# Causal attention inside a decoder trunk: scores laid out with keys on partitions, a separate product pass for the row maxima, row sums by adds on GpSimd

## The chip, the cores and the metric

The kernel runs on one core of one Trainium2 chip. The metric is the device time of one execution in microseconds; the median of several runs counts. Engines: PE is TensorE, DVE is VectorE, ACT is ScalarE, POOL is GpSimd, SP is SyncE (here it only issues DMAs).

## The reference, cut to what matters

One layer on x (1, 2048, 1024) in float32: an input projection, three token mixers (pooling, attention with a forget gate, a state-space layer), gates, an output projection and a layer norm. The change touches the attention:

```python
logf = jax.nn.log_sigmoid(f_logit)                       # (B, S, 8 heads)
fcum = jnp.cumsum(logf, axis=1)
scores = einsum('bqhd,bkhd->bhqk', qi, k) / sqrt(64)     # head dim 64, S = 2048
bias = fcum[query] - fcum[key]                           # per head
logits = jnp.where(key_pos <= q_pos, scores + bias, -inf)
p = jax.nn.softmax(logits, axis=-1)
out = einsum('bhqk,bkhd->bqhd', p, v)                    # then * silu(gate), then w_up_b
...
gates = sigmoid(zg)     # 3 x 1024 columns of the input projection, each with K = 1024
```

## The kernel before

The kernel has three stages with a barrier of all engines between them: `stage_project` (to about 600 us), `stage_attend` (601 to 1530 us) and `stage_merge` (from 1530 us). Products run in fp32r. Every fp32 operand is split into a high half (an ACT copy to fp32r) and a low half (a DVE subtraction), and a product is done as three (high x high, high x low, low x high), or as two passes where both halves of one operand are stacked on partitions 0 to 63 and 64 to 127.

`stage_attend` works head by head. It also computes the gates' projection (24 tiles of 128 columns for each half of the tokens): per head 12 pieces of 24 products of 512 columns, 288 products, which `fill(slot)` spreads between the steps of the attention so that PE has work while other engines prepare its operands. `fill_plan()` fixes how many gate products stand in which slot. The order on each engine is written out by hand, the same order for every head; semaphores tie the engines together. Heads 0 to 3 are phase 0 and heads 4 to 7 phase 1; between the phases x is loaded and split again for the other half of the tokens (`high_x` L1387, `low_x` L1513).

Within a head a loop goes over 16 tiles t of 128 queries:

- `queries(t+1)` (L1566): the scores with queries on partitions, in pieces of up to 512 keys, two products each (k_hh, k_ll), into three banks `s_ps`.
- `logits` (L1451) on DVE: one operation per piece adds the bias of F (`f_row`, or `f_last` with the mask for the last 128 keys), writes the piece to `s_sb` and takes its row maxima; L1478 joins them to `neg_max`.
- `weights_of` (L1395) on ACT: one exp over the whole row with `neg_max` as bias, and with the row's sum as a second result.
- `turn` (L1576): the weights, 128x128 block by block, are transposed on PE (L1584) into `t_ps`; ACT copies the high half out (L1419), DVE subtracts the low half (L1543).
- `values` (L1588), for every two tiles: v (high half on output rows 0 to 63, low half on 64 to 127) times the weights of 256 queries, high and low, into `o_ps`; ACT copies the lower rows (L1366) and DVE adds them (L1481).
- Once per head the 16 row sums of each query are inverted (L1539, 128x16), transposed (L1603) and written to `invT` in HBM. The merge stage multiplies by them (`scale` in `split_y`, L1718).

At a head's end ACT and DVE split the next head's k and q (`split_kq`, L1374 and L1498). GpSimd computes nothing in this stage: it issues the DMAs for k, q, v, F and the outputs.

In `stage_merge` PE works through 8 blocks of 256 tokens: products into `u_ps` (L2063), gating, products into `h_ps` (L2090), layer norm.

Of the kernel before, what the change touches and what calls it, by code (L numbers as in the profile page):

```python
# [25 lines left out]
P = 128  # L26
# [48 lines left out]
class Kept:  # L75


    def __init__(self, nc, ctx, early_at):
# [30 lines left out]
        self.s_sb0 = at("s_sb0", 4, [P, S])  # L109
# [4 lines left out]
        self.y_out = [at(f"y_out{i}", 5, [P, 2 * P], skip=4 * (2 * BANK + i * 2 * P)) for i in range(2)]  # L114
# [11 lines left out]
        self.k_hh = nc.alloc_sbuf_tensor_at("k_hh", [P, S], F32R, offset=late_at)  # L126
# [12 lines left out]
        self.wu_high, self.wu_split, self.scaled = sem("wu_high"), sem("wu_split"), sem("scaled")  # L139
# [6 lines left out]
def stage_project(nc, io, scr, kept, ident, x_hi, x_lo, x_raw, w_hi, w_lo, w_raw):  # L146


    with ExitStack() as ctx:
# [3 lines left out]
        def sem(name):  # L153
# [49 lines left out]
        x_loaded = [sem(f"x_loaded{k}") for k in range(KT)]  # L203
# [8 lines left out]
         f_done, f_stored) = (  # L212
# [5 lines left out]
                "f_exp", "f_ln", "f_done", "f_stored"))  # L218
# [191 lines left out]
        def _(dve):  # L410
# [144 lines left out]
            for hf in range(2):  # L555
# [152 lines left out]
                next_split(2 + hf)  # L708
                if hf == 0:
# [231 lines left out]
        def _(pool):  # L941
# [108 lines left out]
            for hf in range(2):  # L1050
# [20 lines left out]
                if hf == 1:  # L1071
# [18 lines left out]
            pool.wait_ge(f_stored, 16)  # L1090


def fill_plan():

    per_piece = 3 * KT
    total = G_TILES * NCH * per_piece
    steps = [(t, j) for t in range(Q_TILES) for j in range(-(-(t + 1) // 4))]  # L1100
    slots = ["start", *steps, "end", "tail"]
    counts = {s: FILL_BETWEEN for s in steps}
    counts.update({"start": FILL_START, "end": FILL_END, "tail": FILL_TAIL})
    rest = total - sum(counts[s] for s in slots if isinstance(s, str) or s[1])

    rest -= sum(FILL_SHORT)
    for t in range(Q_TILES):
        counts[t, 0] = rest * (t + 1) // Q_TILES - rest * t // Q_TILES
    for t, more in enumerate(FILL_SHORT):
        counts[t, 0] += more  # L1110
    counts[Q_TILES - 2, 0] -= FILL_LAST
    counts[Q_TILES - 1, 0] += FILL_LAST
    ends, splits, done = {s: [] for s in slots}, {s: [] for s in slots}, 0
    splits["head"] = [1]
    for n, s in enumerate(slots):
        before, done = done, done + counts[s]
        for piece in range(before // per_piece, done // per_piece):
            ends[s].append(piece)
            if piece % NCH == NCH - 1 and piece // NCH + 2 <= G_TILES:
                at = W_SPLIT_AT.get(s[0])  # L1120
                splits[(at, 0) if at else "end"].append(piece // NCH + 2)
    assert done == total
    return counts, ends, splits


Q_TILES = S // P
PHASE_HEADS = HEADS // 2
G_TILES = T_GATE // PHASE_HEADS
FILL_SHORT = (9, 6)
W_SPLIT_AT = {1: 4, 5: 8, 9: 10, 12: 14}  # L1130
FILL_START, FILL_END, FILL_TAIL, FILL_BETWEEN, FILL_LAST = 30, 16, 22, 3, 3
S_PIECES = sum(-(-(t + 1) // 4) for t in range(Q_TILES))
PT_USES = 2 + S_PIECES


def stage_attend(nc, io, scr, kept, ident, mask, x_hi, x_lo, x_raw, gw_hi, gw_lo, gw_raw):
# [4 lines left out]
    with ExitStack() as ctx:  # L1141
# [3 lines left out]
        def sem(name):  # L1145
# [3 lines left out]
        sb("k_hh_place", [P, S])  # L1149
        k_hh = kept.k_hh  # L1150
        g_bias = kept.spare("g_bias", 1, [P, T_GATE])
        g_out, y_out = kept.g_out, [y[0:HD] for y in kept.y_out]
        inv_row = kept.y_out[0][HD:HD + Q_TILES, 0:P]
        k_ll, q_st, q_tmp, vT, f_row = kept.k_ll, kept.q_st, kept.q_tmp, kept.vT, kept.f_row
        v_st = sb("v_st", [P, Q_TILES, 2 * HD], F32R)
        s_sb = [kept.s_sb0, sb("s_sb1", [P, S])]
        mx = [kept.spare(f"mx{i}", 3, [P, 5], 32 * i) for i in range(2)]
        f_last = sb("f_last", [P, P])
        neg_max = [kept.spare(f"neg_max{i}", 3, [P, 1], 64 + 32 * i) for i in range(2)]
        row_sum = kept.spare("row_sum", 0, [P, Q_TILES])  # L1160
        row_inv = kept.spare("row_inv", 0, [P, Q_TILES], 4 * Q_TILES)
        o_low = sb("o_low", [HD, 2 * P])
        pt_hi = sb("pt_hi", [P, Q_TILES, 2 * P], F32R)
        assert nc.sbuf_base <= kept.wu_at + 4 * (KT - EARLY_SPLIT) * KT * P
        pt_lo = sb("pt_lo", [P, Q_TILES, 2 * P], F32R)

        s_ps = [ctx.enter_context(nc.psum_tensor(f"s_ps{i}", [P, BANK], F32)) for i in range(3)]
        t_ps = [ctx.enter_context(nc.psum_tensor(f"t_ps{i}", [P, BANK], F32)) for i in range(2)]
        o_ps = ctx.enter_context(nc.psum_tensor("o_ps", [P, 2, 2 * P], F32))
# [6 lines left out]
        y_stored, y_free = sem("y_stored"), sem("y_free")  # L1176
        x2_loaded = [[sem(f"x2_loaded{c}_{k}") for k in range(0, KT, 2)] for c in range(NCH)]
        x_lo_used, early_loaded = sem("x_lo_used"), sem("early_loaded")
        (x2_hi, x2_split, gb_loaded, gb_half, gw_split_hi, gw_split, g_done, g_ready, k_hi,
         kq_low, f_masked, q_hi, s_full, s_free, max_ready, p_ready, t_full, t_hi, t_lo, inv_ready, o_full,  # L1180
         o_low_ready, y_ready) = (
            sem(n) for n in (
                "x2_hi", "x2_split", "gb_loaded", "gb_half", "gw_split_hi", "gw_split", "g_done", "g_ready", "k_hi", "kq_low", "f_masked", "q_hi", "s_full", "s_free", "max_ready",
                "p_ready", "t_full", "t_hi", "t_lo", "inv_ready", "o_full", "o_low_ready", "y_ready"))

        kq_loaded, v_loaded, f_loaded = kept.kq_loaded, kept.v_loaded, kept.row_loaded

        def pieces(t):

            n0 = sum(-(-(a + 1) // 4) for a in range(t))  # L1190
            keys = (t + 1) * P
            return [(n0 + j, j * BANK, min(BANK, keys - j * BANK)) for j in range(-(-keys // BANK))]
# [5 lines left out]
        def pieces_to(t):  # L1198

            return pieces(t)[-1][0] + 1  # L1200

        gates = scr["gateT"].rearrange("(g d p) t -> d p g t", g=3, p=P)
        assert nc.sbuf_base <= kept.wu_at + 4 * (KT - EARLY_SPLIT + 1) * KT * P
# [3 lines left out]
        def _(sp):  # L1207
# [5 lines left out]
            def store(row, now, m2, c):  # L1213
# [3 lines left out]
                             g_out[c][:]).then_inc(g_stored[c], 16)  # L1217

# [6 lines left out]
            for phase in range(2):  # L1225
# [8 lines left out]
                if phase == 1:  # L1234

                    sp.wait_ge(t_full, (HEADS - 1) * PT_USES + 2)
                    sp.wait_ge(y_stored, 16 * ((HEADS - 1) * 9 + 2))
                    load_inv(sp, kept, scr, 0)
                    for i in range(EARLY):
                        sp.dma_start(kept.early_raw[:, i].rearrange("p k c -> p (k c)"), io["w_up"][i]  # L1240
                                     ).then_inc(early_loaded, 16)
                for u in range(2):
                    for c in range(NCH):
# [11 lines left out]
                        if phase == 1 and u == 0 and c == 1:  # L1255
                            sp.wait_ge(s_full, HEADS * S_PIECES)
                            sp.wait_ge(y_stored, 16 * ((HEADS - 1) * 9 + 2))
                            for g in range(YG):
                                for dst, src in ((kept.mix[g], scr["mixT"]), (kept.sil[g], scr["silT"])):
                                    rows = src[g * (D // YG):(g + 1) * (D // YG)].rearrange("(k p) t -> p k t", p=P)  # L1260
                                    sp.dma_start(dst[:], rows[:, :, 0:BLOCK]).then_inc(kept.mix_loaded[g], 16)
                            sp.wait_ge(g_stored[0], 16 * (T_GATE + 2 * KT + 2))
                            sp.dma_start(kept.gate0[:], gates[0][:, :, 0:BLOCK]).then_inc(kept.gate_loaded[0], 16)
# [970 lines left out]
```

## Time and profile before

| | |
|---|---|
| median of 3 runs | 1898.52 us (1897.03 to 1898.54) |
| span of the profiled execution | 1897.9 us |
| PE busy | 1880.5 us, 99% |
| DVE busy | 1123.9 us, 59% |
| ACT busy | 720.4 us, 38% |
| POOL busy | 450.8 us, 24% |
| mean granted TensorE clock | 0.998 |
| `stage_attend` | 601 to 1530 us |

The times are of runs without a profile. The profiled execution has no time of its own beside its span, from its first to its last instruction; the median is 0.6 us above that. "Busy" is time in which at least one instruction of the engine is under way. PE's products overlap (the next one starts before the last one's result has drained), so the cost of a product is the distance between two starts.

### The profile page before, as it was taken

What the parts mean: (1) busy time and instruction counts of PE and PEld (TensorE: products, weight loads), DVE (VectorE), ACT (ScalarE), POOL (GpSimd) and SP (SyncE); (2) the same over time, 40 slices, a digit from 0 to 9 for tenths busy, and PEclk for the clock granted to TensorE, in tenths of its full rate; (3) what the DMA queues carried; (4) which work ended last, traced back from release to release, by engine and by line L of the source; (5) the groups of instructions that cost most, each with busy time, mean ns of one, the idle gap of its engine ahead of it and who ended that gap; (6) DMA issues with size and microseconds to landing.
All of it is one profiled execution on the core that took longest, in us unless ns stands there. A gap on an engine that the chain in (4) does not pass through costs nothing. (4 is left out here: it accounts for less than half of the span.)

```text
span 1897.9 us, 30532 instructions
## 1 busy us (share of the span) xinstructions
PE 1880.5 (99%) x10349; PEld 1611.9 (85%) x10349; DVE 1123.9 (59%) x2370; ACT 720.4 (38%) x1105; POOL 450.8 (24%) x595
## 2 busy tenths in 40 slices
PE   9999999999999999999999999999999999999998
PEld 7888887888887888888888788888888889999997
DVE  5554225564235665746656675565656688766776
ACT  3121013111024565555545655555555542121111
POOL 2948920399000000010100001000010002223322
PEclk9999999999999999999999999999999999999999
DMA  7132235322432143161432714224152486666542
GB/s 197 67 101 89 88 111 186 80 89 89 151 128 100 63 128 85 45 158 57 126 82 68 228 51 133 77 77 131 49 153 74 157 294 199 189 180 183 166 133 89
DMA packets 111335, 230.22 MB, mean 121 GB/s; under 512 B 11544, under 2 KB 61320, under 8 KB 107640
## 3 DMA queue, kind: packets, MB, share of 16 engines
q1 hardware_dynamic: 96752, 168.69, 27.7%
q0 software_dynamic: 13920, 59.46, 11.9%
q10 hardware_dynamic: 576, 1.05, 0.2%
q8 instruction: 38, 0.62, 0.1%
q14 instruction: 49, 0.40, 0.1%
HBM read 159.29 MB, written 69.27 MB: 120 GB/s over the span
## 5 line engine op out<-in xcount | busy, mean ns | idle before, releaser
L1628 PE MATMUL g_ps<-x_hi,w_hi 128*128 128x512 f32 x768 | 305.9, 398 | 0.0
L1628 PE MATMUL g_ps<-x_hi,w_lo 128*128 128x512 f32 x768 | 305.6, 398 | 0.0
L1543 DVE TENSOR_TENSOR pt_lo<-t_ps,pt_hi 128x512 fp32r<-128x512 f32 (+2 forms) x320 | 193.2, 610 | 150.0 <-ACT pt_hi L1419 145.3
L1628 PE MATMUL g_ps<-x_lo,w_hi 128*128 128x512 f32 x768 | 231.7, 406 | 1.2 <-PEq L1664 1.2
L1419 ACT ACTIVATE pt_hi<-t_ps 128x512 fp32r<-128x512 f32 (+2 forms) x320 | 170.6, 533 | 154.8 <-PE t_ps L1584 149.2
L763 PE MATMUL tile_ps<-x_hi,w_hi 128*128 128x512 f32 x720 | 223.7, 392 | 0.1
L763 PE MATMUL tile_ps<-x_hi,w_lo 128*128 128x512 f32 x720 | 221.8, 389 | 0.0
L763 PE MATMUL tile_ps<-x_lo,w_hi 128*128 128x512 f32 x720 | 221.8, 389 | 0.0
L1306 POOL DMA_DIRECT2D mixT<-y_out x63 | 33.8, 536 | 678.5 <-DVE y_out L1487 601.0
L1584 PE MATMUL t_ps<-ident,s_sb 128*128 128x128 f32 x1088 | 173.1, 274 | 2.5 <-DVE v_st L1528 2.5
L1464 DVE CUSTOM_DVE_ANT_0 s_sb<-s_ps,f_row 128x512 f32<-128x512 f32 (+3 forms) x288 | 161.1, 597 | 15.0 <-PE s_ps L1573 15.0
L323 ACT ACTIVATE w_hi<-w_lo_raw 128x1024 fp32r<-128x1024 f32 x47 | 49.9, 1061 | 312.3 <-DMA w_lo_raw<-in_w_tiles 312.3
L1628 PEld LDWEIGHTS g_ps<-x_hi,w_lo 128*128 128x128 f32 x768 | 144.8, 189 | 25.3
L1628 PEld LDWEIGHTS g_ps<-x_hi,w_hi 128*128 128x128 f32 x768 | 145.1, 189 | 24.7
L1398 ACT ACTIVATE s_sb<-s_sb,neg_max 128x128 f32<-128x128 f32 (+15 forms) x128 | 153.3, 1198 | 24.7 <-DVE neg_max L1478 24.6
L1584 PEld LDWEIGHTS t_ps<-ident,s_sb 128*128 128x128 f32 x1088 | 131.9, 140 | 36.2 <-DVE v_st L1528 3.0
L763 PEld LDWEIGHTS tile_ps<-x_hi,w_hi 128*128 128x128 f32 x720 | 134.6, 188 | 29.4 <-issue 1.4
L763 PEld LDWEIGHTS tile_ps<-x_lo,w_hi 128*128 128x128 f32 x720 | 135.2, 188 | 28.2
L763 PEld LDWEIGHTS tile_ps<-x_hi,w_lo 128*128 128x128 f32 x720 | 135.2, 188 | 28.1
L1628 PEld LDWEIGHTS g_ps<-x_lo,w_hi 128*128 128x128 f32 x768 | 137.0, 190 | 23.3 <-PEq L1664 1.3
L2063 PE MATMUL u_ps<-y_hi,wu_hi 128*128 128x256 f32 x512 | 144.1, 281 | 0.8 <-PEq L1141 0.8
L2063 PE MATMUL u_ps<-y_lo,wu_hi 128*128 128x256 f32 x512 | 144.5, 282 | 0.0
(319 smaller groups left out, 3595.5 us busy)
## 6 DMA issues: line engine op xcount, KB each, us to landing
w_lo_raw<-in_w_tiles SPq DMA_DIRECT2D x95, 512.0 KB, 3.7
gateT<-g_out SPq DMA_DIRECT2D x96, 256.0 KB, 3.0
gate<-gateT SPq DMA_DIRECT2D x62, 384.0 KB, 4.7
qkvT<-zout SPq DMA_DIRECT2D x24, 512.0 KB, 3.2
x_lo_raw<-in_xT SPq DMA_DIRECT2D x20, 512.0 KB, 9.7
silT<-zout SPq DMA_DIRECT2D x16, 512.0 KB, 2.7
k_ll<-qkvT POOLq DMA_DIRECT2D x16, 512.0 KB, 7.3
q_st<-qkvT POOLq DMA_DIRECT2D x16, 512.0 KB, 9.2
```

Source lines behind the costliest of these rows:

```text
L323: act.activation(w_hi[par][:], w_raw[par][:], ACT.Copy).then_inc(w_split_hi, 1)
L763: last = pe.matmul(tile_ps[par][:, c * BANK:(c + 1) * BANK], w[par][:, k, :], x[:, k, c * BANK:(c + 1) * BANK], start=(k == 0 and j == 0), ...
L1306: pool.dma_start(scr["mixT"][bass.ds(row, HD), p * 2 * P:(p + 1) * 2 * P], y_out[p % 2]).then_inc(y_stored, 16)
L1398: act.activation(row, row, ACT.Exp, bias=neg_max[t % 2][:], accum_out=row_sum[:, t:t + 1]).then_inc(p_ready, 1)
L1419: act.activation(pt_hi[:, k0 // P:(k0 + keys) // P, (t % 2) * P:(t % 2 + 1) * P], t_ps[n % 2][:, 0:keys].rearrange("p (k q) -> p k q", q=P ...
L1464: return dve.tensor_tensor_reduce(s_sb[t % 2][:, k0 + a:k0 + b], s_ps[n % 3][:, a:b], f, 1.0, -3e38, ALU.subtract, ALU.max, mx[t % 2][:, c ...
L1543: dve.tensor_tensor(pt_lo[part], t_ps[n % 2][:, 0:keys].rearrange("p (k q) -> p k q", q=P), pt_hi[part].bitcast(F32), ALU.subtract).then_i ...
L1584: last = pe.transpose(t_ps[n % 2][:, a * P:(a + 1) * P], s_sb[t % 2][:, k0 + a * P:k0 + (a + 1) * P], ident[:])
L1628: mm = pe.matmul(g_ps[c][:], w[j % 2][:, k, :], x[:, k, c * BANK:(c + 1) * BANK], start=(r == 0), stop=(r == 3 * KT - 1))
L2063: mm = pe.matmul(u_ps[d % 2][:, n, :], w, y[:, k, :], start=(k == k0 and j == 0), stop=(k == k1 - 1 and j == 2))
```

## The change

Scores come with keys on partitions, so that the weights need no transpose before the values. 16 query tiles become four groups g of 512 queries (`Q_GROUPS`, `QG` = 4); a head has 40 steps (g, i), one per group and tile of 128 keys.

- `maxima(g, m)`: one product of the high halves (q_m as weights, k_b moving), with queries on partitions, only to get a row maximum. DVE reduces it in `s_ps` (`tensor_reduce`, and `tensor_tensor_reduce` with the mask for the last 128 keys). It needs to be no exact maximum, since the same shift is applied everywhere. `shifts`: three small DVE operations; `shift_rows`: one PE transpose, and four DVE copies into rows 64 and 65 of q_m, where the shift enters the scores' product as two more rows; F of the keys enters as rows 96 and 97 of k_b. The pieces for group g+1 stand in the steps of group g (`MAX_COUNTS`).
- `scores(n)`: two products (k_b x q_m, k_a x q_low) of up to 512 queries into `st_ps[n % 2]`. `weights` on ACT: exp from `st_ps` to a slot of `p_all` (three slots). `masked` on GpSimd: affine_select on the diagonal block. `high_p` (ACT copy) and `low_p` (DVE subtraction, both inputs in SBUF).
- `add_up` on GpSimd: sums p_all over the key tiles into `acc`. `sums(g)` on PE: ones times acc, high and low, into one of the two banks `s_ps`. Every use of `s_ps` (maxima, shift transposes, sums; `bank_order`) alternates between them.
- `values(n - 2)`: two products into `o_ps[g % 2]`. `low_rows`, `output`: as before, 64x512. `inverse(g)` on DVE: reciprocal of 64x512 out of `s_ps` into `inv`. `scale_y` on GpSimd multiplies, `store_y` stores; no `invT`, and no `scale` in the merge.
- At a head's end: four ACT copies (`high_kq`, before `low_rows` of the last group) and two DVE operations (`low_kq`). In front of the first head begins now wait for the last store of qkvT, and v is loaded only then. F is stored negated and split, by two DVE operations in the projection stage.

```diff
+LAG, RING_P = 2, 3
+FILL_A, FILL_B, FILL_C, FILL_END, FILL_MID, FILL_TAIL = 10, 10, 10, 12, 8, 14
+FILL_SHORT = 8
+MAX_COUNTS = ((3, 3, 2, 0), (2, 2, 2, 2, 2, 2, 0, 0), (2, 2, 2, 2, 2, 2, 1, 1, 1, 1, 0, 0), (0,) * 16)
+def last_step(g):
+    return 2 * (g + 1) * (g + 2) - 1
+SUM_AT = {last_step(g) + LAG + 2: g for g in range(Q_GROUPS - 1)}
...
+            def maxima(at, g, m):                       # PE
+                pe.wait_ge(s_free, at(S_USES, u + 1))
+                pe.matmul(s_ps[u % 2][:, 0:keys], q_m[:, t * P:(t + 1) * P], k_b[:, k0:k0 + keys], start=True,
+                          stop=True).then_inc(s_full, 1)
+            def sums(at, g):                            # PE
+                pe.wait_ge(s_free, at(S_USES, u + 1))
+                pe.wait_ge(acc_split, at(Q_GROUPS, g + 3))
+                pe.matmul(s_ps[u % 2][:], ones[:], acc_hi[:], start=True, stop=False)
+                pe.matmul(s_ps[u % 2][:], ones[:], acc_lo[:], start=False, stop=True).then_inc(s_full, 1)
+            def inverse(at, g):                         # DVE
+                dve.wait_ge(y_ready, at(Q_GROUPS, g + 1))
+                dve.wait_ge(s_full, at(S_USES, u + 1))
+                dve.reciprocal(inv[:], s_ps[u % 2][0:HD]).then_inc(s_free, 1)
+            def low_p(at, n):                           # DVE
+                dve.wait_ge(p_high, at(N_STEPS, n + 1))
+                dve.tensor_tensor(p_lo[:, n % RING_P, q0:], p_all[:, n % RING_P, q0:], p_hi[...], ALU.subtract)
...
+                fill("A")                               # PE, one head
+                # 16 transposes of v
+                for m in range(QG):
+                    maxima(at, 0, m)
+                fill("B")
+                shift_rows(at, 0)
+                fill("C")
+                for n, (g, i) in enumerate(STEPS):
+                    scores(at, n)
+                    if n in SUM_AT:
+                        sums(at, SUM_AT[n])
+                    for m in pieces_at(n):
+                        maxima(at, g + 1, m)
+                    if n == last_step(g) and g + 1 < Q_GROUPS:
+                        shift_rows(at, g + 1)
+                    fill(n)
+                    if n >= LAG:
+                        values(at, n - LAG)
+                fill("end")
+                values(at, N_STEPS - 2)
+                fill("mid")
+                values(at, N_STEPS - 1)
+                sums(at, Q_GROUPS - 1)
+                fill("tail")
...
+                for n, (g, i) in enumerate(STEPS):      # DVE, one head
+                    if n in SUM_AT:
+                        inverse(at, SUM_AT[n])
+                    for m in pieces_at(n):
+                        maxima(at, g + 1, m)
+                    if n:
+                        low_p(at, n - 1)
...
-                    last = pe.transpose(t_ps[n % 2][:, a * P:(a + 1) * P], s_sb[t % 2][...], ident[:])
-                dve.reciprocal(row_inv[:, 0:t + 1], row_sum[:, 0:t + 1]).then_inc(inv_ready, 1)
```

## Rows read from the trace of the kernel before

**Rows 1.** The page: busy time and share of an engine; chain that ended last.
```profile
PE 1880.5 (99%) x10349; PEld 1611.9 (85%) x10349; DVE 1123.9 (59%) x2370; ACT 720.4 (38%) x1105; POOL 450.8 (24%) x595
...
PE u_ps L2063 9%; PE h_ps L2090 8%; PE h_ps L2099 1%; DMA gate<-gateT 0%; DVE wo_lo L1929 0%; DVE gate L1988 0%; DVE wu_lo L1929 0%; DVE gate_first L1988 0%; DVE gate L1996 0%; DVE m_lo L1941 0%; DVE x_t L2040 0%; DVE gate L2000 0%; DVE gate_first L1996 0%; DVE x_t L2047 0%; PE h_ps L2080 0%
```

**Rows 2.** Windows, attention: stretch, length, PE, PEld, DVE, ACT, POOL busy, clock, DMA, GB/s.
```profile
601.00:1530.00 929.00, 926.46 (x5323) 795.93 (x5324) 574.01 (x1598) 524.35 (x849) 62.32 (x113) 1.00 0.36 105
```

**Rows 3.** Timeline of PE, 760 to 764 us: start, duration, line, count.
```profile
760.87 0.39 PE L1628 MATMUL g_ps<-x_hi,w_hi 128*128 128x512 f32 x1
761.10 0.28 PE L1598 MATMUL o_ps<-pt_hi,v_st 128*128 128x256 f32 x1
761.21 0.28 PE L1598 MATMUL o_ps<-pt_lo,v_st 128*128 128x256 f32 x1
...
762.94 0.62 PE L1584 MATMUL t_ps<-ident,s_sb 128*128 128x128 f32 x4
763.32 0.47 PE L1628 MATMUL g_ps<-x_hi,w_lo 128*128 128x512 f32 x1
763.63 0.39 PE L1628 MATMUL g_ps<-x_hi,w_hi 128*128 128x512 f32 x1
```

**Rows 4.** Timeline of PE, the transposes of v in two consecutive heads.
```profile
723.56 1.21 PE L1645 MATMUL t_ps<-ident,vT 64*128 64x64 f32 x16
...
839.08 1.21 PE L1645 MATMUL t_ps<-ident,vT 64*128 64x64 f32 x16
```

**Rows 5.** DVE groups, 620 to 1545 us (count | busy us, mean ns), and one timeline row.
```profile
L1543 DVE TENSOR_TENSOR pt_lo<-t_ps,pt_hi 128x512 fp32r<-128x512 f32 x224 | 154.9, 692 | 113.0 <-ACT pt_hi L1419 108.4
...
L1448 DVE TENSOR_TENSOR w_lo<-w_lo_raw,w_hi 128x1024 fp32r<-128x1024 f32 x46 | 56.3, 1224 | 36.9 <-ACT w_hi L1352 36.9
...
L1464 DVE CUSTOM_DVE_ANT_0 s_sb<-s_ps,f_last 128x128 f32<-128x128 f32 x124 | 35.6, 287 | 26.9 <-PE s_ps L1573 26.3 <-DVE f_last L1456 0.6
...
L1539 DVE RECIPROCAL row_inv<-row_sum 128x16 f32<-128x16 f32 x8 | 2.0, 253 | 11.4 <-ACT s_sb L1398 11.4
...
L1539 DVE RECIPROCAL row_inv<-row_sum 128x2 f32<-128x2 f32 x1 | 0.2, 155 | 0.0
...
581.51 1.28 DVE L663 TENSOR_SCALAR zout<-tile_ps,bias 128x1024 f32<-128x1024 f32 x1 [5.05 <-PE tile_ps L763]
```

**Rows 6.** ACT groups, 620 to 1545 us.
```profile
L1376 ACT ACTIVATE k_hh<-k_ll 128x2048 fp32r<-128x2048 f32 x7 | 13.3, 1902 | 0.0
```

**Rows 7.** DMA issues (KB each, us to landing), and a memset of POOL.
```profile
qkvT<-zout SPq DMA_DIRECT2D x24, 512.0 KB, 3.2
...
vT<-qkvT POOLq DMA_DIRECT2D x8, 512.0 KB, 4.7
...
L1044 POOL MEMSET toep<- 128x2048 f32 x1 | 1.8, 1814 | 0.0
```

**Rows 8.** Timeline of PE and windows (the clock after POOL's column) at the phase change.
```profile
1078.31 0.33 PE L1584 MATMUL t_ps<-ident,s_sb 128*128 128x128 f32 x1 [2.54 <-DVE v_st L1528]
...
1078.30:1079.50 1.20, 1.20 (x6) 1.09 (x7) 1.20 (x6) 0.28 (x1) 0.00 (x0) 1.00 0.41 157
1079.50:1082.90 3.40, 3.40 (x9) 2.62 (x8) 1.37 (x10) 1.18 (x3) 0.00 (x0) 0.50 0.25 90
1082.90:1090.00 7.10, 7.10 (x40) 5.95 (x39) 3.52 (x15) 3.24 (x8) 0.54 (x1) 1.00 0.29 90
```

**Rows 9.** POOL adds in the merge, and POOL beside DVE in the projection (timeline).
```profile
L2117 POOL TENSOR_TENSOR x_t<-x_t,ln_b 128x512 f32<-128x512 f32 x30 | 40.0, 1353 | 1.2
...
187.38 0.91 POOL L1029 TENSOR_TENSOR xs<-xs,zs 128x256 f32<-128x256 f32 x1
188.24 1.89 POOL L1030 TENSOR_TENSOR xw<-xw,scratch 128x256 f32<-128x256 f32 x1
...
187.89 1.47 DVE L421 TENSOR_TENSOR w_lo<-w_lo_raw,w_hi 128x1024 fp32r<-128x1024 f32 x1 [3.12 <-ACT w_hi L323]
```

More of the change, by code:

```diff
@@ L1099, in fill_plan @@
     total = G_TILES * NCH * per_piece
[L1100 to L1112, printed above, removed]
+    slots = ["A", "B", "C", *range(N_STEPS), "end", "mid", "tail"]
+    counts = {"A": FILL_A, "B": FILL_B, "C": FILL_C, "end": FILL_END, "mid": FILL_MID, "tail": FILL_TAIL}
+    for n in range(QG):
+        counts[n] = FILL_SHORT
+    rest, steps = total - sum(counts.values()), N_STEPS - QG
+    for n in range(QG, N_STEPS):
+        counts[n] = rest * (n - QG + 1) // steps - rest * (n - QG) // steps
     ends, splits, done = {s: [] for s in slots}, {s: [] for s in slots}, 0
-    splits["head"] = [1]
-    for n, s in enumerate(slots):
+    splits[1] = [1]
+    for s in slots:
         before, done = done, done + counts[s]
@@ L1119, in fill_plan @@
             if piece % NCH == NCH - 1 and piece // NCH + 2 <= G_TILES:
-                at = W_SPLIT_AT.get(s[0])
-                splits[(at, 0) if at else "end"].append(piece // NCH + 2)
+                later = s + SPLIT_LATER if isinstance(s, int) else "tail"
+                splits[later if later in splits else "end"].append(piece // NCH + 2)
     assert done == total
     return counts, ends, splits
[L1126 to L1133, printed above, removed]
 def stage_attend(nc, io, scr, kept, ident, mask, x_hi, x_lo, x_raw, gw_hi, gw_lo, gw_raw):
@@ L1158, in stage_attend @@
[L1158 to L1167, printed above, removed]
@@ new lines, in stage_attend @@
+        acc_hi, acc_lo = sb("acc_hi", [P, BANK], F32R), sb("acc_lo", [P, BANK], F32R)
+        o_low = sb("o_low", [HD, BANK])
+        y_t = [sb("y_t0", [HD, BANK]), kept.y_last]
+        inv = sb("inv", [HD, BANK])
+        p_hi = sb("p_hi", [P, RING_P, BANK], F32R)
+        p_lo = sb("p_lo", [P, RING_P, BANK], F32R)
+        p_all = sb("p_all", [P, RING_P, BANK])
+        assert nc.sbuf_base <= kept.wu_at + 4 * (KT - EARLY_SPLIT + 1) * KT * P
+        g_bias = kept.spare("g_bias", 1, [P, T_GATE])
@@ L1182, in stage_attend @@
             sem(n) for n in (
[L1183 to L1192, printed above, removed]
+                "x2_hi", "x2_split", "gb_loaded", "gb_half", "gw_split_hi", "gw_split", "g_done", "g_ready", "made", "rows_made", "rows_zero",
@@ L1234, in _ @@
                 if phase == 1:
[L1236 to L1241, printed above, removed]
+                    load_merge()
                 for u in range(2):
@@ L1254, in _ @@
                             load_wo(sp, kept, io["w_out"], 0)
[L1255 to L1263, printed above, removed]
-                            sp.wait_ge(t_full, (HEADS - 1) * PT_USES + pieces_to(Q_TILES - 2) + 2)
-                            sp.wait_ge(g_stored[0], 16 * (T_GATE + 2 * KT + 4))
-                            for d, place in kept.gate_first.items():
-                                sp.dma_start(place[:], gates[d][:, :, 0:BLOCK]).then_inc(kept.gate_loaded[d], 16)
                         if phase == 0 and u == 1 and c == 1:
@@ L1545, in body @@
+                low_p(at, N_STEPS - 1)
+                low_acc(at, Q_GROUPS - 1)
                 for j in splits("end", last):
@@ L1565, in _ @@
         def _(pe):
-            def queries(at, t, part=slice(None)):
-                for n, k0, keys in pieces(t)[part]:
-                    if n >= 3:
-                        pe.wait_ge(s_free, at(S_PIECES, n - 2))
-                    ps = s_ps[n % 3][:, 0:keys]
-                    pe.matmul(ps, q_st[:, t * P:(t + 1) * P], k_hh[:, k0:k0 + keys], start=True, stop=False)
-                    last = pe.matmul(ps, q_st[:, t * P:(t + 1) * P], k_ll[:, k0:k0 + keys], start=False, stop=True)
-                    last.then_inc(s_full, 1)
```

755 lines of the change are left out of this document (429 added, 326 removed).

## The prediction

> **What bounds the kernel now.** First the page's busy shares and the chain that ended last: TensorE (PE) is busy 99% of the span, VectorE (DVE) 59%, and the chain is TensorE's products [rows 1]. Then the windows: in the attention stretch, the only one the change rewrites, PE is busy 926 of 929 us, DVE 574, ScalarE 524, GpSimd 62 [rows 2]. "Busy" doesn't say what a product costs, since neighbours overlap; start to start does [rows 3]. A 512-column fp32r product takes 0.23 us, a 256-column one 0.11 to 0.12, so I take 0.17 for 384 and 0.06 for 128. Four 128-column transposes take 0.38 and make the next product 0.08 late: 0.115 each. One head lasts 839.08 - 723.56 = 115.5 us [rows 4]. Its sum: 288 gate products 66.2, scores (two passes over 17,408 columns) 15.7, values 16.4, 16 transposes of v 1.1, and 16.1 left for 137 transposes. PE is full, so each wait the change adds is paid in full.
>
> **TensorE's work.** A pass over the causal triangle in the new steps is 24 products of 512 columns and four sets of 512, 384, 256 and 128: 24 x 0.23 + 4 x 0.58 = 7.8 us. Per head: gates 66.2, scores 15.7, values 15.7, the new maxima pass 7.8, four row sums of two products 1.8, four transposes of shifts 0.5, v 1.1: 108.8. That saves 6.7 a head; 8 x 108.8 = 870.
>
> **VectorE's work.** What it does to 512 columns takes 0.69, to 128 0.29, to 1024 1.22, so a column costs 1.04 ns [rows 5]. No row shows a long tensor_reduce; one input at one column per step gives 0.69 for 512, and I know no row below that. The exception is the reciprocal. Before, it handles 16 columns a head in 0.253 us; with 2 columns it takes 0.155 [rows 5]: 0.098 for 14 columns, 7.0 ns a column. The change inverts the sum for each of 512 queries, copied over 64 partitions, four times a head: 0.155 + 510 x 0.0070 = 3.7 us each. Bounds: 0.69 (like the other operations) and 4.3; I take 3.7, since both rows are of this very operation. The Trainium skill ("VectorE: DVE Perf Modes", The fixed hardware budget) says that the reciprocal runs through the pipe with a repeat count of 8; 8 x 1.04 ns x 512 would be 4.3 us as an estimate, and the forecast some 15 us later. The row agrees in kind (6.7 times a normal column).
>
> DVE per head: lower halves of the weights 24 x 0.69 + 4 x 1.97 = 24; maxima 24 full pieces, 16 masked ones of 128 columns (0.29 and 0.08 for the result) and what lies beside these, 27; reciprocals 15; splits of six w tiles, k, q and v 7.3 + 4.4 + 1.4 = 13; outputs and sums 8 x 0.69 = 6; shifts 6: 91 us. That is less than 108.8, but unevenly spread, and DVE works in order.
>
> **Where PE stops.** The maxima, the shift transposes and the sums share two banks in turn, and each use waits until DVE is through with the use two before.
> - Steps 7 and 15 (the sums of groups 0 and 1): PE does the sum, one maxima product, and for the next it needs the bank of the sum, so the reciprocal must end. It starts 0.39 after the second sum product starts and lasts 3.7, with 0.2 for two handovers and some backlog: 4.3; PE has 0.46 of work. Stop 4.0. Behind it wait the gate products, the values and the next scores. 16 x 4.0 = 64.
> - Step 27 (group 2's sum, no maxima): the lower half of step 26 is ready 5.65 after the step begins, PE wants it at 4.3 (step 27 takes 2.6, then 0.46 of scores and 1.23 of gates): 1.4 each, 11 in all. The reciprocal ends at 4.95 there, the subtraction takes 0.69.
> - Steps 0 and 1 issue three maxima products at once for two banks: 0.7 + 0.5 a head, 10.
> - End of a head, T = last scores. ScalarE splits w, does a gate at T+4.6, then four copies of 2048 columns for the next q and k at 1.9 each [rows 6] to T+12.3, and only then o_low to 12.9. DVE: output 13.6, reciprocal 17.4. PE has end, mid, tail and A fills and v's transposes to T+13.7; its second maxima product needs the sum's bank: 3.6. Then DVE splits v (1.4) before the first maxima, so the third and fourth products wait 1.6 and 0.6. 5.8 a head; 6 x 5.8 = 35.
> - Phase change: the new x is split on DVE after that reciprocal, 16 x 0.69, and the third maxima product waits behind all of it. A's products wait for the first split to T+18.1 (8 late), the maxima to T+29.8 (8 more): 16.
> - First head: q, k and v wait for the last qkvT store, which takes 3.2, and v's load another 4.7 [rows 7], against 30 gate products as cover before and 10 now; two memsets of GpSimd at 1.8 stand ahead of v's load. v lands at about 609.7, where PE is through with its cover at 603.2. ScalarE's four copies, from 603.9 on, end at 611.5 and its copy of v at 612.7, DVE's half of v at 613.4, and PE then issues the fourth maxima product at 614.5, 10 later than it could: 10.
> - Last head: PE's warm products wait for the last reciprocal: 2.
>
> **The clock.** Before has one stop of this kind: PE idle 2.54 us at the phase change; 1.2 us after it has restarted the granted clock is 0.50 (1.2 GHz) for 3.4 us, then 1.00 again [rows 8]. That costs 1.7. Stops of 4 us should do the same: 16 at steps 7 and 15, 6 at heads' ends and 2 at the first head and the phase change: 24 x 1.7 = 41. Bounds: nothing, and more than one fall in the long ones (+10).
>
> **What costs nothing.** GpSimd: an add of 512 columns takes 1.35 [rows 9]. Per head 24 of them (32), the 16 shorter ones (14), 16 masks of 128 columns at no more than 0.9 (14), four multiplications (5) and the DMAs (5) are 70 us of 108.8; the three slots of p_all give it two steps of slack. ScalarE has an exp and a copy per step, 1.3 us; a step of PE is 2.15 to 2.6. Were the adds twice as slow, they would set the steps of group 3 (2.7 against 2.15): some 8 us a head. The two operations on F in the projection (2048 columns, 2.2 each) fit in the 5.05 us that DVE idles behind them [rows 5]; without it they would delay a tile by 4.4 once. In the merge two multiplications a block go from DVE, where PE's products are the chain [rows 1]: nothing.
>
> **Sum.** 870 + 10 + 64 + 11 + 35 + 16 + 10 + 2 + 41 = 1059 against 929 now [rows 2]: +130. The profiled execution spans 1897.9, the median is 1898.5, 0.6 above: 1898.5 + 130 = 2028 us.
>
> **The rivals.**
> - The stop is no longer at the reciprocal: it streams like a copy, 0.69. For: every other one-input row does. Against: the two reciprocal rows. Steps 7 and 15 then stop 0.9 (14 in all), step 27 not, a head's end 2.9 (17), phase change 13, first head 10, two clock falls 3: 870 + 10 + 14 + 17 + 13 + 10 + 3 = 937, +8: 1906.
> - Faster: TensorE stays the bound. It is one mechanism: DVE frees each bank in the shadow of PE's other work. 870 plus first head and phase change, 26, is 896: -33, 1865. It decides at 33/8 = 4 us of stops a head, so the reciprocal would have to be under about 1 us and the head's end nearly covered. For: DVE's 91 us (79 with cheap reciprocals) fit in 108.8. Against: the order of the two banks.
> - GpSimd and VectorE block each other. Before, attention leaves GpSimd idle; now its adds run beside DVE's subtraction of two SBUF tiles in every step. In the projection such a pair shows: DVE's w_lo takes 1.47 for 1.22, and the GpSimd operation beside it 1.89 where the one before took 0.91 [rows 9]. With 0.25 on DVE it fits in the slack. If each of DVE's 40 waits out a whole add (1.35), groups 1 and 2, where DVE has least to spare, take 6 and 7 us more: 100 in all, 2128. The Trainium skill ("SBUF — State Buffer", Who interferes with whom) states that a VectorE instruction with two SBUF inputs contends with a GpSimd instruction that reads SBUF, and that whoever comes first holds the shared port for the whole instruction; the rows agree that there is a loss.
> - The clock does not fall: 1987, inside the forecast's own range.
>
> **Chances.** The forecast 0.67 (own range 1965 to 2065), blocking 0.10, cheap reciprocal 0.11, faster 0.12. The range 1906 to 2080 leaves out the faster case and the worse half of the blocking. A measurement of this kernel tells 0.2% (4 us) from no change: faster 0.12, same 0.03 (the lower edge of the cheap reciprocal), slower 0.85.
>
> **What would show it.** PE's span in attention near 1060 for 929 with its work near 870. RECIPROCAL of 64x512 at 3.7 us, x32, and PE idle some 4 us just after each in steps 7 and 15, released by DVE's inv; if it takes under 1 us, the forecast is wrong. Granted clock 0.50 for 3 us after those stops: windows below 1.00 two or three times a head. DVE's 128x512 subtraction well above 0.69 would show the blocking, and a stop at PE's values released by p_lo. From head to head near 130 us (108.8 and the stops) for 115.5 now.

## The result, and the profile after

The changed kernel takes 2093.9 us (median; 2093.3 to 2095.4), the kernel before 1898.5 beside it: ratio 1.103, 95% interval 1.102 to 1.105. It is slower, as forecast, but by 195 us and not by 130; the forecast 2028 is 66 us low and the range ended 14 below the result. The profiled execution spans 2093.7 us.

Nearly all of it is in attention. From the first gate product to the first product of the merge the trace of before has 930.4 us (600.9 to 1531.2) and that of after 1123.8 (601.3 to 1725.1); from there to the end it is 366.7 and 368.6. The page's busy shares and the windows answer to [rows 1, 2] (columns as there):

```profile
PE 1917.3 (92%) x9156; PEld 1583.1 (76%) x9156; DVE 1350.5 (65%) x2055; ACT 739.0 (35%) x1177; POOL 934.0 (45%) x1044
```

```profile
601.00:1725.00 1124.00, 961.92 (x4132) 765.57 (x4132) 809.62 (x1295) 543.99 (x923) 546.69 (x564) 0.93 0.26 77
```

TensorE was busy 926 of 929 us and is now busy 962 of 1124, with fewer instructions. Its clock fell from 1.00 to 0.93. VectorE has 236 us more and GpSimd 484 more. Next, the nine largest entries of TensorE's waits over the whole run (who waits, at which line, for whom: us in total, times, longest). Before, TensorE waited 2.5 us once in attention for VectorE, at the phase change [rows 8], and nowhere else in it above 1.2.

```profile
PE s_ps L1740 <- DVE inv L1642: 79.5, 22, 4.0
PE s_ps L1740 <- DVE mx L1593: 16.6, 16, 4.6
PE o_ps L1775 <- DVE p_lo L1620: 15.1, 14, 1.9
PE st_ps L1764 <- DVE q_m L1614: 11.7, 15, 1.1
PE u_ps L2221 <- PEq L1181: 9.8, 1, 9.8
PE s_ps L1786 <- DVE mx L1588: 8.4, 16, 0.6
PE g_ps L1811 <- DVE x_lo L1678: 7.4, 1, 7.4
PE s_ps L1740 <- DVE mx L1588: 6.7, 8, 0.8
PE st_ps L1826 <- DMA vT<-qkvT: 6.3, 1, 6.3
```

The first line is the stop that the forecast rests on. Here is one, at step 7 of the first head: TensorE's timeline, then VectorE's, then windows (the clock stands after POOL's column).

```profile
642.86 0.49 PE L1786 MATMUL s_ps<-acc_hi,ones 128*128 128x512 f32 x1 [0.56 <-DVE mx L1588]
643.18 0.39 PE L1787 MATMUL s_ps<-acc_lo,ones 128*128 128x512 f32 x1
643.41 0.39 PE L1740 MATMUL s_ps<-k_b,q_m 128*128 128x512 f32 x1
647.57 0.80 PE L1740 MATMUL s_ps<-k_b,q_m 128*128 128x512 f32 x1 [3.77 <-DVE inv L1642]
...
649.45 0.63 PE L1811 MATMUL g_ps<-x_hi,w_lo 128*128 128x512 f32 x1
649.87 0.63 PE L1811 MATMUL g_ps<-x_hi,w_hi 128*128 128x512 f32 x1
```

```profile
642.90 0.75 DVE L1620 TENSOR_TENSOR p_lo<-p_all,p_hi 128x512 fp32r<-128x512 f32 x1
643.58 0.67 DVE L1633 TENSOR_TENSOR y_t<-o_ps,o_low 64x512 f32<-64x512 f32 x1
644.18 3.34 DVE L1642 RECIPROCAL inv<-s_ps 64x512 f32<-64x512 f32 x1
```

```profile
644.00:646.00 2.00, 0.00 (x0) 0.00 (x0) 2.00 (x2) 0.00 (x0) 0.78 (x1) 0.85 0.00 0
646.00:648.00 2.00, 0.43 (x1) 0.43 (x2) 2.00 (x2) 0.00 (x0) 0.00 (x0) 0.50 0.00 0
648.00:650.00 2.00, 2.00 (x6) 1.52 (x6) 1.35 (x3) 0.00 (x0) 0.00 (x0) 0.50 0.00 0
650.00:654.00 4.00, 4.00 (x15) 3.23 (x14) 1.40 (x5) 1.12 (x2) 0.73 (x2) 0.72 0.00 0
```

From 643.41 to 647.57 TensorE starts nothing, while VectorE's reciprocal runs from 644.18 to 647.52. The listed idle time is 3.77 because the product before is drawn 0.39 long; what the stop costs is start to start less one pitch, 4.16 - 0.23 = 3.93. The clock is already at half while TensorE stands still, and stays there for some 5 us after it restarts: products follow at 0.42 instead of 0.23. The sum itself came late too (0.56). VectorE's and GpSimd's groups in attention answer to [rows 5, 9]:

```profile
L1620 DVE TENSOR_TENSOR p_lo<-p_all,p_hi 128x512 fp32r<-128x512 f32 x224 | 254.7, 1143 | 65.5 <-ACT p_hi L1514 64.9
L1588 DVE TENSOR_REDUCE mx<-s_ps 128x1 f32<-128x512 f32 x192 | 128.0, 680 | 89.2 <-PE s_ps L1740 89.1
L1642 DVE RECIPROCAL inv<-s_ps 64x512 f32<-64x512 f32 x32 | 106.8, 3338 | 0.0
```

```profile
L1390 POOL TENSOR_TENSOR acc<-acc,p_all 128x512 f32<-128x512 f32 x192 | 287.2, 1496 | 190.1 <-ACT p_all L1504 182.5 <-POOL p_all L1370 4.4
```

The subtraction of the same form that took 0.69 us [rows 5] takes 1.14. From head to head it is now 136.7 us where [rows 4] has 115.5:

```profile
745.95 1.22 PE L1826 MATMUL st_ps<-ident,vT 64*128 64x64 f32 x16
...
882.64 1.22 PE L1826 MATMUL st_ps<-ident,vT 64*128 64x64 f32 x16
```

### The profile page after: what moved, and what is told of

It reads as the page before. It is cut to its first block and busy times, and to the rows that moved or that the text cites. A ratio compares the mean times of both kernels' runs of the same rounds, so it can differ in the third digit from the quotient of the medians.

```text
span 2093.7 us, 29293 instructions
## 1 busy us (share of the span) xinstructions
PE 1917.3 (92%) x9156; PEld 1583.1 (76%) x9156; DVE 1350.5 (65%) x2055; ACT 739.0 (35%) x1177; POOL 934.0 (45%) x1044
## 5 line engine op out<-in xcount | busy, mean ns | idle before, releaser
L1390 POOL TENSOR_TENSOR acc<-acc,p_all 128x512 f32<-128x512 f32 (+3 forms) x288 | 363.0, 1261 | 207.7 <-ACT p_all L1504 182.5
L1620 DVE TENSOR_TENSOR p_lo<-p_all,p_hi 128x512 fp32r<-128x512 f32 (+1 forms) x320 | 300.0, 941 | 98.1 <-ACT p_hi L1514 95.5
L1504 ACT ACTIVATE p_all<-st_ps 128x512 f32<-128x512 f32 (+1 forms) x320 | 170.8, 534 | 456.7 <-PE st_ps L1765 419.8
L1811 PE MATMUL g_ps<-x_hi,w_hi 128*128 128x512 f32 x768 | 314.2, 409 | 0.0
L1740 PE MATMUL s_ps<-k_b,q_m 128*128 128x512 f32 (+2 forms) x320 | 113.8, 415 | 102.8 <-DVE inv L1642 79.5
L1588 DVE TENSOR_REDUCE mx<-s_ps 128x1 f32<-128x512 f32 x192 | 128.0, 680 | 89.2 <-PE s_ps L1740 89.1
L1514 ACT ACTIVATE p_hi<-p_all 128x512 fp32r<-128x512 f32 (+1 forms) x320 | 179.0, 559 | 9.8 <-POOL p_all L1370 9.8
L1811 PEld LDWEIGHTS g_ps<-x_lo,w_hi 128*128 128x128 f32 x768 | 151.7, 203 | 40.0 <-issue 8.0
L1811 PEld LDWEIGHTS g_ps<-x_hi,w_hi 128*128 128x128 f32 x768 | 152.6, 199 | 32.3 <-issue 0.4
L1740 PEld LDWEIGHTS s_ps<-k_b,q_m 128*128 128x128 f32 x320 | 65.5, 208 | 129.1 <-DVE inv L1642 86.2
```

What stands on the lines that cost most here:

```text
L1390: pool.tensor_tensor(total[:, q0:], total[:, q0:], p_all[:, n % RING_P, q0:], ALU.add).then_inc(acc_done, 1)
L1504: act.activation(p_all[:, n % RING_P, q0:], st_ps[n % 2][:, q0:], ACT.Exp).then_inc(p_exp, 1)
L1514: act.activation(p_hi[:, n % RING_P, q0:], p_all[:, n % RING_P, q0:], ACT.Copy).then_inc(p_high, 1)
L1588: dve.tensor_reduce(into[:, column:column + 1], ps[:, 0:keys], AX_X, ALU.max).then_inc(s_free, 1)
L1620: dve.tensor_tensor(p_lo[:, n % RING_P, q0:], p_all[:, n % RING_P, q0:], p_hi[:, n % RING_P, q0:].bitcast(F32), ALU.subtract).then_inc(p_l ...
L1740: pe.matmul(s_ps[u % 2][:, 0:keys], q_m[:, t * P:(t + 1) * P], k_b[:, k0:k0 + keys], start=True, stop=True).then_inc(s_full, 1)
```

## The experiments

Each is the changed kernel with one edit unless said otherwise. "Attention" is first gate product to first product of the merge; "half" is time at the granted clock 0.50 in whole stretches inside it, with their number (the changed kernel and seven of the others have one more, which its end cuts). The runs of before beside them had medians of 1896.9 to 1897.5. Each time is of two runs, of four for the changed kernel and "interleaved"; the interval of a ratio is 0.002 to 0.004 to either side, 3 to 8 us. The last column is the mean duration of one.

The expectations set two accounts against each other. In the "bank theory" the loss is TensorE's wait for a bank that VectorE's reciprocal holds, and the half clock behind it. In the "blocking theory" it is GpSimd's adds, which slow VectorE's subtraction.

| kernel | us | ratio | attention | half, stretches | 128x512 subtraction |
|---|---|---|---|---|---|
| changed | 2093.9 | 1.103 | 1123.8 | 153.6, 25 | 1.14 |
| reciprocal as a copy | 1995.9 | 1.052 | 1026.6 | 71.7, 15 | 1.11 |
| a quarter of the reciprocal | 2030.1 | 1.070 | 1055.9 | 109.2, 21 | 1.10 |
| busy during steps 7, 15 | 2064.3 | 1.088 | 1093.8 | 71.7, 10 | 1.15 |
| and at heads' ends | 2067.7 | 1.090 | 1095.9 | 71.7, 11 | 1.15 |
| adds without a read | 2064.1 | 1.088 | 1092.5 | 129.7, 25 | 0.76 |
| copy, and adds without a read | 1961.4 | 1.034 | 991.3 | 47.8, 8 | 0.73 |
| order at a head's end | 2069.9 | 1.091 | 1098.3 | 133.1, 19 | 1.15 |
| that, and small sums | 1973.7 | 1.040 | 1003.8 | 34.1, 7 | 1.17 |
| that, interleaved | 1970.3 | 1.039 | 1000.1 | 30.7, 8 | 1.17 |
| that, adds without a read | 1945.6 | 1.025 | 976.9 | 20.5, 3 | 0.69 |

**The reciprocal as a copy.** Leaves the inversion out.

```diff
-                dve.reciprocal(inv[:], s_ps[u % 2][0:HD]).then_inc(s_free, 1)
+                dve.tensor_copy(inv[:], s_ps[u % 2][0:HD]).then_inc(s_free, 1)
```

> The reciprocal of 64x512 is replaced by a copy of the same size at the same place, so the sums are not inverted (the output is wrong by that). Bank theory (the reciprocal holds the bank that TensorE needs next, and the clock falls after the stop): RECIPROCAL 3.34 us becomes a copy of about 0.68; the stops at steps 7 and 15 shrink by 2.66 each (43 in all), step 27's 2.1 goes (17), the end of a head loses 2.66 (21), and most of the 26 stretches at clock 0.50 in attention go (50 to 80 us): 1935 to 1965 us. Blocking theory (GpSimd's adds and VectorE's subtraction block each other and set the pace): the subtraction stays at 1.14 us and the time stays above 2050.

**A quarter of it:** the reciprocal on 128 columns, the copy on 384.

> Only the first 128 of the 512 columns are inverted, the other 384 are copied (left out: the inversion of those). Bank theory: 0.95 + 0.55 = 1.5 us instead of 3.34, each stop 1.8 shorter: 24 x 1.8 = 44 us less, and the clock falls after fewer or shorter stops (25 to 60 more): 1990 to 2025 us, between the copy and the changed kernel. Blocking theory: as with the copy, above 2050.

Measured 1995.9 and 2030.1: the second 5 us over its window, both below the 2050 of the blocking theory, though the subtraction stays at 1.11 and 1.10. The stop follows the reciprocal's length: 79.5 us of waits, 35.6, 20.8 for 3.34, 1.42 and 0.67 us of VectorE. This one instruction, 32 times, is worth 98 us, half the loss. The copy lands 31 us over its own, and 22 waits of up to 1.3 us are left: VectorE comes late even to a short operation. From the kernel with the copy, TensorE's waits:

```profile
PE s_ps L1740 <- DVE inv L1642: 20.8, 22, 1.3
```

**Busy during the stop.** At steps 7 and 15 the maxima product behind the sum is issued 18 times; each repeat writes the same values.

```diff
+                for _ in range(17 if u - 1 in (BANK_USE["sum", 0], BANK_USE["sum", 1]) else 0):
+                    pe.matmul(s_ps[u % 2][:, 0:keys], q_m[:, t * P:(t + 1) * P], k_b[:, k0:k0 + keys], start=True, stop=True)
```

> At steps 7 and 15 the maxima product behind the sum is issued 18 times into the same bank (same result), 17 x 0.23 = 3.9 us, so that TensorE is busy where it waited for the reciprocal. If the clock's fall follows TensorE's idling and costs what the windows say: the stretches at 0.50 go from 26 to about 10, each had 3.4 to 6.8 us at half speed, so 16 x 2.6 = 42 us less: 2045 to 2060. If the clock costs nothing because TensorE waits anyway, or falls nevertheless: 2094 within 10.

Measured 2064.3, 4 us over the upper end. The stop is as long as before, only filled, and the clock stays at 1.00 behind it (timeline, then windows over the same place):

```profile
643.99 4.13 PE L1741 MATMUL s_ps<-k_b,q_m 128*128 128x512 f32 x17
647.96 0.68 PE L1742 MATMUL s_ps<-k_b,q_m 128*128 128x512 f32 x2
```

```profile
646.00:650.00 4.00, 4.00 (x19) 3.10 (x18) 3.58 (x4) 0.00 (x0) 0.00 (x0) 1.00 0.00 0
```

82 us less at half clock are worth 29.6 us: 0.36 us per us. By that rate the 153.6 us of the changed kernel cost 55, an estimate, since the rate comes from the stops at steps 7 and 15 alone.

**And at heads' ends:** the same, and the head's first maxima product 14 times.

> The repeated maxima products of the earlier run stay at steps 7 and 15, and the head's first maxima product is now issued 14 times as well, so that TensorE also runs through the wait for the last row sum's reciprocal at the end of each head. With repeats at steps 7 and 15 alone there were 10 stretches at half the clock, 71.7 us, most of them at heads' ends, and going from 153.6 to 71.7 us had been worth 29.5 us of time, 0.36 us per us. If the clock's price at the heads' ends is the same: at most 4 stretches, under 35 us at half clock, and 2064 - 0.36 x 40 = 2050 (2043 to 2056). Rival, the stretches at the heads' ends run beside waits that last anyhow and cost nothing: the stretches go and the time stays, 2060 to 2068. If the repeats themselves delay the products behind them, over 2068.

Measured 2067.7, stretches as before. The time lies in the rival's window, but the stretches did not go, so it does not speak for the rival. My repeats were sized wrongly: this product has 128 columns and 13 of them last 1.5 us, so half of each stop was left open and the clock fell behind it all the same. Here the clock falls behind stops of 1.47 and 1.02 us close together (timeline; the pitch behind them is 0.43). What the clock costs at heads' ends stays open.

```profile
881.22 1.67 PE L1741 MATMUL s_ps<-k_b,q_m 128*128 128x128 f32 x13
882.72 0.28 PE L1742 MATMUL s_ps<-k_b,q_m 128*128 128x128 f32 x1
884.47 0.39 PE L1742 MATMUL s_ps<-k_b,q_m 128*128 128x256 f32 x1 [1.47 <-DVE inv L1642]
885.87 1.01 PE L1742 MATMUL s_ps<-k_b,q_m 128*128 128x384 f32 x2 [1.02 <-DVE mx L1593]
886.68 0.63 PE L1813 MATMUL g_ps<-x_hi,w_hi 128*128 128x512 f32 x1
887.11 0.63 PE L1813 MATMUL g_ps<-x_hi,w_lo 128*128 128x512 f32 x1
```

**Adds without a read.** GpSimd's adds into the row sums become memsets of the same tile, so the sums are not formed.

```diff
-                    pool.tensor_tensor(total[:, q0:], total[:, q0:], p_all[:, n % RING_P, q0:], ALU.add).then_inc(acc_done, 1)
+                    pool.sem_inc(passed)
+                    pool.memset(total[:, q0:], 1.0).then_inc(acc_done, 1)
```

> GpSimd's adds of p_all into acc are replaced by memsets of acc of the same width, which read nothing from SBUF (the row sums are left out). Blocking theory: VectorE's 128x512 subtraction goes from 1.14 to 0.69 us and 80 us or more are won: below 2015. Bank theory: the subtraction goes to 0.69 too, but only the waits on it (15 us), part of the waits for maxima banks (0.7 at each of 16 sums) and a few clock stretches go: 2055 to 2080, with the stops behind the reciprocal still at 4 us.

**With the copy as well:**

> Two edits at once: the reciprocal of 512 columns is a plain copy (alone: 1996), and GpSimd's 24 adds a head are memsets that read nothing (alone: 30 us less). The scale and the row sums are wrong by that, the work of the other engines is the same. If the stop at the reciprocal and the slowing of VectorE by GpSimd's adds are separate costs they add up: 1996 - 30 = 1966 (1960 to 1973), and VectorE's subtraction of 128x512 falls from 1.11 to about 0.7 us. If the adds cost time mainly because VectorE comes late to the reciprocals, most of that is gone already with the copy: 1980 to 1994. If the stop hid part of the blocking, less than 1958.

Measured 2064.1 and 1961.4, the first inside the bank theory's window, the second inside that of separate costs. VectorE's subtraction is nearly back at the 0.69 of [rows 5]:

```profile
L1621 DVE TENSOR_TENSOR p_lo<-p_all,p_hi 128x512 fp32r<-128x512 f32 x224 | 170.2, 762 | 113.6 <-ACT p_hi L1515 112.9
```

The adds are worth 30 us alone and 34 beside the copy: separate costs, they add up. In the first of the two the 8.4 us of waits at the row sums are gone from the list, those for p_lo fall from 15.1 to 10.0, those for q_m from 11.7 to 8.4. A memset is also shorter than an add (0.53 for 1.50 us), so the edit's 30 us alone can't tell contention from a GpSimd that is simply done sooner. But TensorE never waits for GpSimd in the list above, and what became shorter on VectorE is the instruction itself. The single instructions settle what lengthens it. In the changed kernel the 17 of 224 subtractions beside which no GpSimd instruction ran took 0.68 to 0.69 each; the other 207 average 1.18 and reach 1.78. Without the adds' reads, the 131 subtractions beside a memset alone take 0.69 each too, and those that are still long, up to 1.77, stand beside the one two-input operation left on GpSimd, the multiplication of y.

**Order at a head's end.** ScalarE's o_low comes between the second and third of its four copies; VectorE takes the inverse before k's low half and the first maxima before v's.

```diff
-                    high_kq(at(64, 128))
+                    high_kq(at(64, 128), (0, 1))
...
                 low_rows(at, Q_GROUPS - 1)
+                if not last:
+                    high_kq(at(64, 128), (2, 3))
```

> Only the order at a head's end changes: ScalarE copies o_low between the second and the third of the four copies for the next head, VectorE inverts the last sums before k's lower half and does the first maxima of the next head before v's lower half. Bank theory: VectorE's order makes TensorE stop some 6 us at each of seven heads' ends; about half of it goes (7 x 3 = 21 us) and with it up to seven stretches at half clock of 3.4 to 6.8 us (10 to 20 us): 2050 to 2065. If the end of a head was limited by VectorE's amount of work and not by its order: 2094 within 8.

Measured 2069.9, 5 us over the upper end and 16 below the rival's window: 24 us for order alone. A head's end in the changed kernel, then in this one:

```profile
883.78 0.33 PE L1740 MATMUL s_ps<-k_b,q_m 128*128 128x128 f32 x1
887.03 0.39 PE L1740 MATMUL s_ps<-k_b,q_m 128*128 128x256 f32 x1 [2.92 <-DVE inv L1642]
888.43 1.21 PE L1740 MATMUL s_ps<-k_b,q_m 128*128 128x384 f32 x2 [1.02 <-DVE mx L1593]
```

```profile
879.54 0.50 PE L1750 MATMUL s_ps<-k_b,q_m 128*128 128x128 f32 x2
881.80 0.96 PE L1750 MATMUL s_ps<-k_b,q_m 128*128 128x384 f32 x2 [1.76 <-DVE mx L1599]
```

**Small sums,** on top of that order: the row sums are formed with the 128 queries of a tile on partitions, so that the reciprocal has 4 columns; TensorE turns the result back with four transposes, and VectorE, not GpSimd, multiplies the output.

```diff
-                pe.matmul(s_ps[u % 2][:], ones[:], acc_hi[:], start=True, stop=False)
+                    pe.matmul(out, acc_hi[:, q], ones[:, 0:HD], start=True, stop=False)
...
-                dve.reciprocal(inv[:], s_ps[u % 2][0:HD]).then_inc(s_free, 1)
+                dve.reciprocal(inv4[:], s_ps[u % 2][:, 0:QG * HD].rearrange("p (t c) -> p t c", t=QG)[:, :, 0]).then_inc(s_free, 1)
+                dve.tensor_copy(inv_b[:], inv4[:].unsqueeze(2).broadcast_to([P, QG, HD])).then_inc(inv_made, 1)
```

> The changed kernel with the order of the last experiment and a small reciprocal: the sums come out with queries on partitions (acc as weights, 64 columns of ones), VectorE inverts 128x4, copies it to 64 columns, TensorE transposes it back into the bank, and VectorE multiplies y there instead of GpSimd. All is computed. Bank theory: VectorE holds the bank 0.2 us instead of 3.34, the stops at steps 7, 15 and 27 go, most of the clock stretches too; left are the three-in-a-row maxima, the first head and the phase change: 1915 to 1945. Blocking theory: GpSimd's adds still slow the subtraction to 1.1 us and the time stays above 1960.

**Interleaved:** also three gate products between maxima products where three or four follow each other.

> As e5_small0, and gate products stand between maxima products where three or four follow each other on two banks (steps 0 and 1, head's start). Bank theory: the 1.1 and 0.7 us stops there go, 8 x 2.5 = 20 us less than e5_small0: 1895 to 1925, about the kernel before. Otherwise the same as e5_small0.

**And adds without a read,** the row sums left out again:

> As e5_small, with GpSimd's adds replaced by memsets of the same width (the row sums are left out). Bank theory: with the stops gone TensorE is nearly full, the subtraction at 0.69 instead of 1.1 us takes what little is left: 0 to 25 us below e5_small. Blocking theory: 30 us or more below e5_small.

Measured 1973.7, 1970.3 (ratio 1.0385, 1.0368 to 1.0403) and 1945.6. The long stop is gone, replaced by these (VectorE's groups and TensorE's waits of the interleaved kernel):

```profile
L1642 DVE COPY inv_b<-inv 128x256 f32<-128x256 f32 x32 | 15.1, 473 | 1.1
L1640 DVE RECIPROCAL inv<-s_ps 128x4 f32<-128x4 f32 x32 | 5.2, 163 | 0.0
```

```profile
PE st_ps L1779 <- DVE q_m L1614: 14.9, 15, 1.1
PE s_ps L1803 <- DVE mx L1588: 8.0, 16, 0.5
PE st_ps L1859 <- DMA vT<-qkvT: 5.9, 1, 5.9
PE s_ps L1755 <- DVE inv L1640: 4.7, 15, 0.4
```

That is 124 us better than the change, 120 of it without the interleaving, and still 3.9% slower than before. The expectations were missed: 1973.7 is 29 us over the 1915 to 1945 of the bank theory and above the 1960 of the blocking theory, and 1970.3 is 45 over 1925, where I had expected it about level with before. Interleaving is worth 3 us, which is inside the intervals. Leaving the adds' reads out gives another 25, at the upper edge of the bank theory's 0 to 25, and 48 us over before remain. Neither theory is enough by itself.

Two things stand behind this. The stops that remain are many and short, nearly all for VectorE. And the small sums give back half of the 54 us of TensorE's work that the layout saves. Timeline of the interleaved kernel, two of eight sum products and the four transposes:

```profile
640.22 0.28 PE L1803 MATMUL s_ps<-ones,acc_hi 128*128 128x64 f32 x1
640.33 0.28 PE L1804 MATMUL s_ps<-ones,acc_lo 128*128 128x64 f32 x1
642.99 0.60 PE L1815 MATMUL s_ps<-ident,inv_b 128*64 128x128 f32 x4
```

A product of 64 columns follows the one before after 0.11 and a transpose after 0.10, so that these twelve take 1.28 us where two products of 512 columns took 0.46: 26 us for 32 sums. The row sums are left out in the last kernel, but these products are not. So the 48 us are the price of this version, and not of the layout. None of these versions beats the kernel before.

## Why the prediction was right in sign and short in size

Terms in us of start-to-start time over one pitch (the usual distance between two starts); the forecast's working stands above. It failed in three places: it put GpSimd's adds at nothing, it left short hand-overs between VectorE and TensorE without a price, and it took every stretch at half clock for 3.4 us.

| step | forecast | trace |
|---|---|---|
| TensorE's work | 870 | 872 |
| steps 0, 1 | 10 | 14 |
| steps 7, 15 | 64 | 65 |
| step 27 | 11 | 16 |
| heads' ends | 35 | 28 |
| phase change | 16 | 12 |
| first head | 10 | 9 |
| last head | 2 | 10 |
| row sums wait for a bank | none | 11 |
| group boundaries wait for q_m | none | 15 |
| clock, and what is left | 41 | 72 |
| attention | 1059 | 1124 |

**Right: the work and the main stop.** 872 is 8 x 109, a head's period less every start-to-start time above its pitch. The reciprocal of 512 columns takes 3.34 for 3.7; by 64x128 at 0.94 us and 64x512 at 3.34 it is 6.25 ns a column. The stop comes out at 4.0 as forecast because VectorE starts on it 1.0 us after the second sum product starts (644.18 less 643.18), where I had 0.39: two sizes that were off cancelled, by luck. The Trainium skill ("VectorE: DVE Perf Modes", The fixed hardware budget) gives a repeat count of 8; against 1.04 ns for a normal column [rows 5] the runs show 6.0, so the count does not carry over to the time, and the 4.3 us estimated from it is 1.0 too long. The rival "cheap reciprocal" was given by its condition alone: with a reciprocal made as cheap as a copy the kernel takes 1996, and not its 1906, so that rival's time was wrong too. The waits at row sums and group boundaries that the forecast lacks stay in that run (8.3 and 12.9 us).

**Wrong: "What costs nothing", GpSimd.** I gave the adds nothing and blocking a rival of its own. It is neither: not each of 40 waiting out a whole add (2128), but not nothing. Measured, leaving their reads out is worth 30 us in the changed kernel and 25 in the one without long stops. It enters where VectorE was counted as having slack: the waits at row sums (gone without the adds), at values, at group boundaries. VectorE was busy 101 us a head in attention (809.6 over 8), and not 91. The Trainium skill ("SBUF — State Buffer", Who interferes with whom) has a VectorE instruction with two SBUF inputs contend with a GpSimd instruction that reads SBUF, and not with one that only writes it. The runs agree: 1.14 us against 0.69, and 0.69 beside memsets, while the 128x512 maxima, which read PSUM, take 0.68 beside the same adds.

**Wrong: "unevenly spread, and DVE works in order" was written and then not priced.** The chains at group boundaries (last maxima, shift, q_m, next scores) and the sum's own wait for its bank are 26 us that I had no term for. They are not all blocking: 8.4 of 11.7 us of waits for q_m stay without the adds. The 30 us of the adds are no further row of the table; they lie in these rows, in step 27's and in the clock's.

**Wrong: the clock, 24 x 1.7 = 41.** The count was right (25 stretches), the length not: I took the one stretch of [rows 8], 3.4 us, for all; most last 6.8 and some 10.2, 153.6 in all. By the rate of the filled stop that is 55; added up over the products that ran in these stretches, the start-to-start time above the pitch at full clock is 53. What is left of the 72, 17 us, is not located: short gaps of under 0.7 us, which the other rows of the table leave out, may be in it.

**Wrong, small: the last head.** I counted the reciprocal, not the end of the stage behind it. GpSimd's multiplication of y runs to 1718.4, and TensorE goes on at 1725.1:

```profile
1725.10 0.55 PE L2221 MATMUL u_ps<-y_hi,wu_hi 128*128 128x256 f32 x1 [9.75 <-PEq L1181]
```

With the multiplication on VectorE (small sums) this wait is 1.9; what fills the 6.7 us after GpSimd is done I did not test. Heads' ends (28 for 35), the phase change (12 for 16) and the first head (9 for 10) were over, which hid 12 of the 77 us that the other terms were under.

## What to carry to other kernels

Before work is taken off a full engine by giving it to engines with idle time, follow each bank that both use through one period: a saving of 6.7 us a head on TensorE was bought with four reciprocals that hold one of two banks for 3.3 us each. Invert before you spread (4 columns, then a copy), not after (512): that, with the multiplication of y moved from GpSimd to VectorE, was worth 96 us here, and the order that puts the releasing instruction first another 24. Count what the new form costs the full engine: short products gave 26 us of TensorE's saving back. And when an engine that is busy 72% of the time is asked to answer within half a microsecond many times a period, price its lateness, at every hand-over and not only at the long instruction.

## What the runs showed of the hardware

- A stop of TensorE of 3.8 us: the granted clock is 0.50 before it restarts, and for about 5 us after. The half-clock stretches of the changed kernel last 3.4, 6.8 or 10.2 us, and in one place two stops of 1.5 and 1.0 us with one product between them have one behind them too. Filling a stop with repeated products keeps 1.00.
- VectorE's reciprocal: 6.25 ns a column in fp32 (64x128 0.94, 64x512 3.34), with 128x4 at 0.16.
- GpSimd's 128x512 add beside VectorE: 1.50 us against 1.35 in the merge [rows 9]; VectorE's subtraction pays more, 0.45 us each. At the phase change it is the other way round: GpSimd's multiplication of 64x512, 1.3 to 2.2 us in other places, starts beside 16 subtractions in a row, takes 10.61 and ends 1.1 us after them, while they follow each other after 0.60:

```profile
1163.17 9.64 DVE L1678 TENSOR_TENSOR x_lo<-x_lo_raw,x_hi 128x512 fp32r<-128x512 f32 x16
1163.33 10.61 POOL L1396 TENSOR_TENSOR y_last<-y_last,inv 64x512 f32<-64x512 f32 x1 [13.33 <-DVE inv L1642]
```

- Products of 64 columns follow each other after 0.11 us, where 512 columns take 0.23.
